# Two streams of 512 and 256 tokens multiplied as two pieces of 384 columns, one PSUM bank each

## The reference, cut to what matters

```
for l in range(2):
    hc = rmsnorm(ctx) * (1 + csc1) + csh1          # context, same weights
    hx = rmsnorm(x) * (1 + sc1) + sh1              # latents
    y  = token_mixers(h @ w_in[l], ...)            # retention, Fourier, short convolution
    x  = x + g1 * (y_x @ w_out[l]);  x = x + g2 * conv_ffn(norm(x), ...)
    if l == 0: the same two updates for ctx
out = rmsnorm(x, final_norm_g)

def conv_ffn(h, w_up, w_conv, w_down):
    u = dwconv3(h @ w_up, w_conv)                  # 3 taps along the tokens, per stream
    val, gate = split(u);  return (val * silu(gate)) @ w_down    # hidden width 2816
```

## Time and profile before

| | |
|---|---|
| median of 3 runs | 1590.44 us (1586.62 to 1593.49) |
| the profiled execution: its own time | 1588.05 us |
| its span, first to last instruction | 1586.3 us |
| PE busy, share of the span | 1538.2 us, 97% |
| PEld busy | 1294.0 us, 82% |
| DVE busy | 945.9 us, 60% |
| POOL busy | 897.2 us, 57% |
| ACT busy | 340.7 us, 21% |
| mean granted clock of TensorE | 0.992 |

### The profile page before, as it was taken

How to read it: one execution, slowest core, us unless ns; L and a number is a source line. 1 busy time by engine, 2 the same in 40 slices (tenths; PEclk the granted TensorE clock), 3 DMA queues, 4 the chain that set the end, 5 groups by cost and what they waited for, 6 DMA issues and landing times.

```text
span 1586.3 us, 24348 instructions
## 1 busy us (share of the span) xinstructions
PE 1538.2 (97%) x8994; PEld 1294.0 (82%) x8994; DVE 945.9 (60%) x1326; ACT 340.7 (21%) x528; POOL 897.2 (57%) x841
## 2 busy tenths in 40 slices
PE   7999999899999999999999999999999999999997
PEld 5888887787888888888888878877778888888886
DVE  4698575677787847882488547377556431341344
ACT  4332112314221001110012225121324220220221
POOL 2456342564655645554555546564485777767773
PEclk9999999999999999999999999999999999999999
DMA  9345111442333433332333223232132223223322
GB/s 384 133 136 183 54 41 41 133 147 76 120 123 128 143 123 116 109 119 67 118 119 120 93 77 108 68 107 67 54 107 67 93 92 106 93 93 107 105 89 97
DMA packets 50081, 172.72 MB, mean 109 GB/s; under 512 B 6240, under 2 KB 8800, under 8 KB 48992
## 3 DMA queue, kind: packets, MB, share of 16 engines
q1 hardware_dynamic: 47616, 167.79, 31.3%
q10 hardware_dynamic: 2400, 4.05, 0.8%
HBM read 165.52 MB, written 2.10 MB: 106 GB/s over the span
## 4 chain that ended last, share of the span: by engine, by line
PE 82%; DVE 11%; ACT 2%; DMA 2%; issue 1%; POOL 1%; SPq 1%; ACTq 0%; DVEq 0%
PE pair L1362 74%; PE pair L1475 3%; DVE qxi L1121 1%; DVE nt L966 1%; DVE h_lo L972 1%; DVE vz L1102 1%; DVE h_lo L1199 1%; DMA start_slot<-in_start_mods 1%; DVE aux L825 1%; PE aux L1712 1%; PE aux L1718 1%; PE aux L1699 1%; PE aux L1500 1%; DVE state L1110 1%; DMA rot<-kT 1%
## 5 line engine op out<-in xcount | busy, mean ns | idle before, releaser
L508 POOL TENSOR_SCALAR w_hi<-raw 128x512 fp32r<-128x512 f32 (+1 forms) x410 | 295.3, 720 | 620.2 <-PE pair L1362 502.0
L510 POOL TENSOR_TENSOR w_lo<-raw,w_hi 128x512 fp32r<-128x512 f32 (+1 forms) x410 | 587.3, 1432 | 34.3
L1362 PE MATMUL pair<-h_hi,w_hi 128*128 128x512 f32 x1760 | 530.5, 359 | 9.9 <-DVE mid L1217 4.7
L1362 PE MATMUL pair<-h_lo,w_hi 128*128 128x512 f32 x1760 | 524.8, 356 | 0.9 <-DVE h_lo L1199 0.7
L1362 PE MATMUL pair<-h_hi,w_lo 128*128 128x512 f32 x1760 | 523.7, 355 | 0.0
L1362 PEld LDWEIGHTS pair<-h_hi,w_hi 128*128 128x128 f32 x1760 | 287.9, 189 | 66.2 <-issue 6.1
L1362 PEld LDWEIGHTS pair<-h_lo,w_hi 128*128 128x128 f32 x1760 | 288.7, 189 | 52.2 <-DVE h_lo L1199 2.0
L1362 PEld LDWEIGHTS pair<-h_hi,w_lo 128*128 128x128 f32 x1760 | 287.5, 189 | 46.9
L825 DVE CUSTOM_DVE_ANT_0 aux<-mod_slot,c_b 128x1024 f32<-128x1024 f32 x160 | 225.0, 1406 | 4.5 <-DMA mod_slot<-in_mods 1.8
L1255 DVE SCALAR_TENSOR_TENSOR x<-pair,modv,x 128x256 f32 (+3 forms) x84 | 53.0, 658 | 177.8 <-PE pair L1362 177.6
L1362 PE MATMUL pair<-hid_lo,w_hi 128*128 128x512 f32 x486 | 147.5, 358 | 0.0
(11 more groups left out here) (171 smaller groups left out, 1301.1 us busy)
## 6 DMA issues: line engine op xcount, KB each, us to landing
raw<-in_slabs SPq DMA_DIRECT2D x206, 512.0 KB, 3.5
mod_slot<-in_mods SPq DMA_DIRECT2D x80, 512.0 KB, 3.5
start_slot<-in_start_mods SPq DMA_DIRECT2D x8, 1024.0 KB, 15.3
x<-in_x SPq DMA_DIRECT2D x4, 768.0 KB, 10.0
out<-fin SPq DMA_DIRECT2D x16, 128.0 KB, 1.9
rot<-kT ACTq DMA_DIRECT2D x16, 64.0 KB, 3.7
rot<-Y ACTq DMA_DIRECT2D x16, 64.0 KB, 3.2
rot<-kT SPq DMA_DIRECT2D x16, 64.0 KB, 2.0
```

The lines of the kernel that those rows point to most:

```text
L508: nc.gpsimd.tensor_scalar(w_hi[p][:, a:b], raw[p][:, a:b], 1.0, 1.0, ALU.mult, ALU.mult).then_inc(split, 1)
L510: nc.gpsimd.tensor_tensor(w_lo[p][:, a:b], raw[p][:, a:b], w_hi[p][:, a:b].bitcast(fp32), ALU.subtract).then_inc(split, 3 if narrow(s) else 1)
L1362: ins = nc.tensor.matmul(out[:, a:b], wt, xt[:, a:b], start=first and k == 0, stop=last and k == 2)
```

## The change

Where both streams are multiplied with the same weights, `cols` becomes two pieces of 384 columns: columns 0 to 383 go to the first bank of the pair and columns 384 to 767 to the second. The latents' last 128 columns then lie in the second bank, ahead of the context. Readers of such a pair use a two-piece access pattern (`in_halves`, `halves`) in the same number of instructions. There are two exceptions on DVE, where one tap or one gate goes with one stream or one shift: in `outer_taps` of layer 0 each latent instruction is cut in two at column 384 (six instructions in place of four), and in `residual` of layer 0 the latent instruction is cut in two (three in place of two). The stages that multiply stream by stream are left as they were. The first hidden block of layer 0 belongs to them, so it stands ahead of its loop with its four tap instructions.

```diff
+HALF = TC // 2
+BANK = 512
+    def in_halves(p, ncol):
+        return pair[p][:, :].rearrange("p (i c) -> p i c", i=2)[:, :, 0:HALF] if ncol == TC else pair[p][:, 0:ncol]
+    def halves(ap, ncol):
+        return ap.rearrange("p (i c) -> p i c", i=2) if ncol == TC else ap
+    def pieces(a, b, ncol):
+        if ncol < TC:
+            return [(a, b, a)]
+        cuts = [(a, min(b, HALF), a)] if a < HALF else []
+        return cuts + ([(max(a, HALF), b, BANK + max(a, HALF) - HALF)] if b > HALF else [])
...
@@ hidden(i, first), ACT
-                        nc.scalar.activation(tv[:, 0:nlat], pair[0][:, 0:nlat], ACT.Copy, scale=vec_dyn("ffnw", w))\
+                        nc.scalar.activation(kept(tv), made(0), ACT.Copy, scale=vec_dyn("ffnw", w))\
...
@@ residual, DVE
-                                nc.vector.scalar_tensor_tensor(
-                                    x[:, 2 * i + p, a0:a1], pair[p][:, a0:a1], modv[:, st, bass.ds(2 * i + (c0 + p), 1)],
-                                    x[:, 2 * i + p, a0:a1], ALU.mult, ALU.add)\
-                                    .then_inc(drained[p] if st == 0 else ctx_ready, 1)
+                                for a, b, at_ in pieces(a0, a1, nlat):
+                                    ins = nc.vector.scalar_tensor_tensor(
+                                        x[:, 2 * i + p, a:b], pair[p][:, at_:at_ + b - a],
+                                        modv[:, st, bass.ds(2 * i + (c0 + p), 1)], x[:, 2 * i + p, a:b], ALU.mult, ALU.add)
+                                ins.then_inc(drained[p] if st == 0 else ctx_ready, 1)
...
@@ outer_taps, DVE
-                                ops += [(t[:, a0 + 1:a1], pair[p][:, a0:a1 - 1], 0),
-                                        (t[:, a0:a1 - 1], pair[p][:, a0 + 1:a1], 2)]
+                                for shift, tap in ((1, 0), (-1, 2)):
+                                    for a, b, at_ in pieces(a0 + (shift < 0), a1 - (shift > 0), 0 if by_stream else nlat):
+                                        ops.append((t[:, a + shift:b + shift], pair[p][:, at_:at_ + b - a], tap))
...
+                    alone = 1 if l == 0 and g == 0 else 0
+                    if alone:
+                        hidden_block(0, None, True)
...
@@ products, PE
                     for a, b in cols:
-                        ins = nc.tensor.matmul(out[:, a:b], wt, xt[:, a:b], start=first and k == 0, stop=last and k == 2)
+                        place = BANK if a == HALF else a
+                        ins = nc.tensor.matmul(out[:, place:place + b - a], wt, xt[:, a:b], start=first and k == 0,
+                                               stop=last and k == 2)
...
-                both, lat = [(0, T), (T, TC)], [(0, T)]
+                both, lat = [(0, HALF), (HALF, TC)], [(0, T)]
```

More of the change, by code:

```diff
@@ L677, in copy_out @@
                     act.wait_ge(done, slab + 1)
-                    nc.scalar.activation(dst, pair[p][:, 0:ncol], ACT.Copy).then_inc(drained[p], 1)
+                    by_stream = l == 1 and slab < PLAN[1, "kv"] + 2
+                    nc.scalar.activation(dst if by_stream else halves(dst, ncol),
+                                         pair[p][:, 0:ncol] if by_stream else in_halves(p, ncol), ACT.Copy)\
+                        .then_inc(drained[p], 1)
                 def swap(src, slab, unit):
@@ L723, in gate @@
                         act.wait_ge(s["y_ready"], j - 1)
-                    nc.scalar.activation(sg[p][:, 0:nlat], pair[p][:, 0:nlat], ACT.Silu).then_inc(drained[p], 1)
+                    nc.scalar.activation(halves(sg[p][:, 0:nlat], nlat), in_halves(p, nlat), ACT.Silu)\
+                        .then_inc(drained[p], 1)
                 n = 0
@@ L790, in hidden, with made, kept @@
                     def hidden(i, first):
+                        by_stream = l == 0 and first
+                        def made(p):
+                            return pair[p][:, 0:nlat] if by_stream else in_halves(p, nlat)
+                        def kept(t):
+                            return t[:, 0:nlat] if by_stream else halves(t[:, 0:nlat], nlat)
                         act.wait_ge(done, s0 + 1 + 2 * i)
@@ L794, in hidden @@
                         w = (l * 2 * NHB + u) * 3 + 1 + 3 * i
-                        nc.scalar.activation(tv[:, 0:nlat], pair[0][:, 0:nlat], ACT.Copy, scale=vec_dyn("ffnw", w))\
+                        nc.scalar.activation(kept(tv), made(0), ACT.Copy, scale=vec_dyn("ffnw", w))\
                             .then_inc(s["tv_ready"], 1)
                         act.wait_ge(done, s0 + 2 + 2 * i)
-                        nc.scalar.activation(tg[:, 0:nlat], pair[1][:, 0:nlat], ACT.Copy,
+                        nc.scalar.activation(kept(tg), made(1), ACT.Copy,
                                              scale=vec_dyn("ffnw", w + 3 * NHB)).then_inc(s["tg_ready"], 1)
@@ L1136, in _ @@
                             dve.wait_ge(done, slab + 1)
-                            nc.vector.tensor_tensor(z[:, b, 0:nlat], pair[1][:, 0:nlat], z[:, b, 0:nlat], ALU.mult)\
+                            nc.vector.tensor_tensor(halves(z[:, b, 0:nlat], nlat), in_halves(1, nlat), halves(z[:, b, 0:nlat], nlat),
+                                                    ALU.mult)\
                                 .then_inc(drained[1], 1)
@@ L1287, in _, with hidden_block @@
                     s0 = PLAN[l, "up", g]
[L1288 to L1291, removed]
+                    per = 2 * (5 if l == 0 else 1) + (2 * MODS_UP if l == 0 else 0)
+                    def hidden_block(i, base, by_stream):
                         def outer_taps(t, p, w):
@@ L1330, in _ @@
                             .then_inc(s["hid_ready"], 1)
-                    assert steps[0] - start == per, (steps[0] - start, per)
-                    steps[0] = start + n * per
+                    alone = 1 if l == 0 and g == 0 else 0
+                    if alone:
+                        hidden_block(0, None, True)
+                    start = steps[0]
+                    steps[0] = start - alone * per
+                    with dve.Fori(alone, n) as i:
+                        hidden_block(i, i * per, False)
+                    assert steps[0] - start == per - alone * per, (steps[0] - start, per)
+                    steps[0] = start + (n - alone) * per
                     if l == 0:
```

## The result

The changed kernel is slightly slower: 1598.47 us median against 1589.88, 12 runs each, a ratio of 1.0053 with a 95% interval of 1.0041 to 1.0065. That is 8.4 us, between 6.5 and 10.3. The direction was forecast and the time lies in the range, but the loss is only a little over half of the 15 us that were worked out.

What follows compares the result with a forecast made beforehand. The prediction took TensorE as the bound, with DVE equally full in layer 0's up stage. It added 17.6 us there, less 2.6 us gained outside, about +15 us on 1590.4, giving 1606 us, range 1583 to 1626.

Steps and rivals of the forecast that it cites:

- DVE's ring as the second bound: Layer 0's up stage: DVE's repeating work per hidden block, 16.94 us, is as full as TensorE's 16.96 us.
- 0.25 us for an extra instruction: DVE's cut taps in layer 0: each added instruction costs 0.25 us, 1.0 us more per block.
- The stall behind POOL: DVE held up by POOL's splits in layer 0's up stage: stays at 1.6 us per block, period 18.0 us.
- the stepping of the ring against the splits: Layer 0's up stage: splits every 4.24 us still meet a DVE reduction or addition in each half block.
- The end of a group: Last block of an up group: `hid_lo` about 2 us later, `last_late` covers about 1; 1 us more in groups 1 and 2.
- TensorE's couples: Two matmuls covering 768 columns: 350 ns with `h` instead of 353, 352 ns with `hid`, unchanged.
- the 2.6 us that were forecast: Outside layer 0's up stage: 864 couples with `h` gain 3 ns each, 2.6 us in total.
- `residual` at nothing: Layer 0's `residual`: one more DVE instruction per slab, 0.25 us, costs nothing beside an 8.5 us slab; uncovered, 7 us.
- the ring was not absorbed (1): Rival: in layer 0's up stage DVE's stall absorbs the added taps, period 16.96 us; 1588 us, chance 0.19.
- Rival 2: TensorE's equal pieces take 346 ns a couple and DVE keeps up, period 16.6 us or less; 1575 us, chance 0.09.
- Rival 3: TensorE's short matmul waits for its weight load, which 384 columns would cover; 1564 us, chance 0.05.
- Rival 4: TensorE's pieces get slower, 360 ns a couple, 10 us lost outside the up stage; 1618 us, chance 0.17.

Runs made afterwards that it cites:

- whole taps (3): Changed kernel, each tap reading its columns in one instruction where they lay before (wrong columns, same lengths): 1584.39 us against 1590.94 for the kernel before, ratio 0.9957.
- own product buffer (4): Changed kernel with cut taps, product of value and gate in its own buffer instead of `tv`: 1581.98 us against 1590.94 for the kernel before, ratio 0.9942.
- Runs 1: Kernel before, only the latent taps of layer 0's hidden blocks cut at column 384: 1603.17 us against 1590.94, ratio 1.0073.
- Run 2: Changed kernel, layer 0's up slabs back to 512 and 256 columns with whole taps: 1587.46 us against 1590.94 for the kernel before, ratio 0.9974.
- the two traces of before: Kernel before, its first trace and one more unedited execution, 1594.56 us; the changed kernel was likewise executed once more, 1598.74 us.
- run 6: Kernel before with the product of value and gate in its own buffer: 1589.62 us against 1591.41, ratio 0.9989.
- run 9: Kernel before, the 256 context columns of each couple multiplied ahead of the 512 latent columns: 1588.43 us against 1589.85, ratio 0.9994.
- run 5: Kernel before, latent taps of layer 0's hidden blocks cut at columns 192 and 384: 1621.42 us against 1591.41, ratio 1.0176.

## Why the prediction came out as it did

The stages of layer 0's hidden part, from the first matmul of each to the first of the next (us):

| | up 0 | down 0 | up 1 | down 1 | up 2 |
|---|---|---|---|---|---|
| before | 118.82 | 67.41 | 118.71 | 58.98 | 118.72 |
| changed | 121.87 | 67.93 | 120.58 | 59.84 | 120.01 |
| changed, whole taps (3) | 116.61 | 67.58 | 116.48 | 59.34 | 116.48 |
| changed, own product buffer (4) | 116.59 | 67.58 | 116.48 | 59.14 | 116.48 |

- *DVE's ring as the second bound*: right, and the cause. Runs 1, 3 and 4 show it from three sides: the taps alone cost it, whole taps give it back, and a shorter ring carries the cut taps.
- *0.25 us for an extra instruction*: right, 0.62 + 0.35 us in place of 0.75, and 0.04 us between them.
- *The stall behind POOL*: the term that was mis-sized. It was kept at 1.6 us, for a period of 18.0. It fell to 1.07, for 17.47. The step that failed is the stepping of the ring against the splits, which let "one or the other reduction or addition" be met in each half of the block; in most blocks only the reductions behind the `tv` taps are held up, by 0.9 and 1.2 us in turns, and nothing behind the `tg` taps is. The mean period of 17.47 us lies just inside the 17.4 to 18.6 that were forecast. The up stages lost 3.05 + 1.87 + 1.29 = 6.2 us, where the sum had 6.2 + 9.4 = 15.6. With the measured period the same sum gives 3.1 us for group 0 and 2.1 each for the others.
- *The end of a group*: forecast 1 us for groups 1 and 2; the down stages behind groups 0 and 1 are 0.5 and 0.9 us longer, and the one behind group 2 0.5 us. So of the 17.6 us that were added for ring and ends the first trace shows 8.1.
- *TensorE's couples*: 350 ns was forecast for `h` and 346.7 measured, the lower bound. For `hid`, 352 was right. The gain outside the up stage is then 864 x 6.6 ns = 5.7 us on paper. Not all of it arrives. The 1.1 us ahead of the slab wait at 126 us are lost there, which the prediction did not see, and in the first trace of before the 144 couples of the out slabs had nothing to gain. Run 2 is 4.1 us (1.9 to 6.2) faster, but 2.2 us of that are its third up group, if all its executions ran that group as the traced one did; some 2 us are left. Runs 3 and 4 gain 6.7 us in the up stages of their 6.8 and 9.2, which leaves 0.1 and 2.5. So the 2.6 us that were forecast agree with this by luck of two errors: the gain of a couple was put at half, and all of it was taken to arrive.
- *`residual` at nothing*: no wait of TensorE for it shows in the changed trace. It was not tried alone.
- *The rivals*: the ring was not absorbed (1), and DVE did not keep up (2). Rival 2 named the right condition, though: 384 columns are worth 0.4 to 0.6% as soon as the ring runs at 16.6 us (runs 3 and 4). Rival 3, the weight load: overhead of 13.3 ns stays on each 384-column matmul, as on 512 columns alone. The 325 ns for a couple that the prediction estimated from the Trainium skill ("TensorE: Matmul & The Clock Gate", "Back-to-back issue gap") are not reached; the page gives its 2.5 ns over the columns for an isolated matmul, and this is a stream with a weight load for each. Rival 4, slower couples, is out.

The two traces differ by 9.2 us: 6.2 in the up stages, 1.9 in the down stages, and 1.1 in the rest: 1.6 us more by the first of the key and value slabs and 0.9 in them, less 1.5 us behind them. The first two vary as much between two traces of one kernel. The first whole slab of keys and values starts at 46.6 and 46.0 us in the two traces of before and at 48.3 and 46.9 in those of the changed kernel; from there to the first matmul of the retention (L1675 before, L1720 after the change) it is 113.9 and 118.1 us before, 114.8 and 117.2 in the changed kernel. So the 1.1 us are within what chance does, and the 2.6 us of gain forecast outside the up stages cannot be seen in these two traces.

## What to carry to other kernels

An engine at 60% of the span can be full in one stage. Compare its period there with that of the engine that sets the end, and look at what its idle time waits for: if nothing of it waits for the bound, every added instruction counts, and a faster bound gains nothing. When a change makes the bound engine faster and adds fixed costs to its neighbour, look first for a wait inside the neighbour's ring that a separate buffer removes; here one such buffer, worth nothing by itself, turned 0.5% slower into 0.6% faster.

## What the runs showed of the hardware

DVE's stall behind GpSimd's splits is elastic. It was 1.56 us in a block before, 1.07 with 1.0 us more work, and about 1.6 in the fourth run, where DVE had time to spare. In the sixth run, where the ring needs 1.26 us less and TensorE keeps its pace, it is 2.5 us: reductions of 1496 ns on the mean, additions of 597, and `hid_lo` at 1639 in place of 960. Such a stall is no fixed cost and should not be carried over into a changed schedule. That it is one behind the splits is read from instructions that lie side by side; no run took the splits away.

The rate of a couple depends on more than its lengths, and what else was not found. In run 2, the same loop of 512 and 256 columns took 1.07 us for three couples in group 1 and 1.03 us in group 2, with the same operands' buffers:

```profile
640.41 0.51 PE L1406 MATMUL pair<-h_hi,w_hi 128*128 128x512 f32 x2
...
641.48 0.51 PE L1406 MATMUL pair<-h_hi,w_hi 128*128 128x512 f32 x2
...
840.22 0.50 PE L1406 MATMUL pair<-h_hi,w_hi 128*128 128x512 f32 x2
...
841.25 0.51 PE L1406 MATMUL pair<-h_hi,w_hi 128*128 128x512 f32 x2
```

Over the whole group it is 116.48 us in place of 118.72, exactly the time of 384 and 384 columns. So 6.6 ns of a couple's overhead can be absent with unequal pieces too. It was so in one of the 15 up groups with these lengths in which TensorE set the pace (before twice, runs 2, 6 and 9); run 9 shows that the order of the two is not what decides.

Outside the up groups it changes from one execution to another of the same kernel. These are the out slabs of layer 0, three couples in 1.04 us in the first trace of before and in 1.06 in the second:

```profile
320.46 0.51 PE L1362 MATMUL pair<-h_hi,w_hi 128*128 128x512 f32 x2
...
321.50 0.51 PE L1362 MATMUL pair<-h_hi,w_hi 128*128 128x512 f32 x2
```

```profile
323.96 0.53 PE L1362 MATMUL pair<-h_hi,w_hi 128*128 128x512 f32 x2
...
325.02 0.53 PE L1362 MATMUL pair<-h_hi,w_hi 128*128 128x512 f32 x2
```

Run 9 has 1.04 us there too, and run 6 has it in the first key and value slabs, where it took 78.45 us to the wait, as with equal pieces. So a stretch of unequal pieces runs at one of two rates, and the gain of equal pieces depends on which of them the kernel before happened to have. With equal pieces the 6.6 ns were absent in every stage that multiplies `h`.

The granted clock fell in an up stage in one trace only, that of run 5. It stood at 0.50, which is 1.2 GHz, from 465.5 to 472.3 us and from 718.1 to 721.5, and began to fall both times while TensorE waited for `tv`, for 3.83 and 2.40 us. The first one, the end of the wait and one microsecond of TensorE's (length, busy time and matmuls, granted clock, share and rate of the DMAs):

```profile
466.97 1.01 PE L1364 MATMUL pair<-h_hi,w_hi 128*128 128x512 f32 x2 [3.83 <-DVE tv L1302]
```

```profile
470.00:471.00 1.00, 1.00 (x5) 0.50 0.20 33
```

So a late neighbour can cost the bound engine its clock as well as the wait.
